# A two-block transformer kernel in fp32 on one core: a ninth weight slot, new buffers in the expert stage, and another order of ScalarE's work

## What is computed

```
def reference(...):
    x = first_block(x, ...)      # 2 x: x + hybrid_layer(x): one wide projection (3488 columns), four mixers
                                 #      (latent attention, short convolution, spatial gate, block attention),
                                 #      each gated by silu, and a projection back
    return second_block(x, ...)

def second_block(x, c, ...):
    c_act = silu(c)
    for i in range(2):
        sh1, sc1, g1, sh2, sc2, g2 = split(c_act @ ada_w[i] + ada_b[i])        # ada_w: 1024 x 6144
        h = x * (1 + sc1) + sh1
        y = neighbourhood_mixer(h, ...) if i == 0 else gqa_mixer(h, ...)       # 16 heads of 64
        x = layer_norm(ALPHA * x + (1 + g1) * y, ln_g[i, 0], ln_b[i, 0])
        h = x * (1 + sc2) + sh2
        y = hierarchical_moe(h, ...)                                           # 32 experts, 2 per token
        x = layer_norm(ALPHA * x + (1 + g2) * y, ln_g[i, 1], ln_b[i, 1])
    return x
```

## Time and profile before

| | |
|---|---|
| median of 3 runs | 1589.41 us (1588.25 to 1590.89) |
| the profiled execution, its own time | 1588.65 us |
| its span, first to last instruction | 1586.9 us |
| PE, DVE, ACT, POOL busy | 88%, 36%, 14%, 6% of the span |
| moved by DMA | 533.32 MB, mean 336 GB/s |
| mean granted TensorE clock | 0.945 |

### The profile page before, as it was taken

One profiled execution on the slowest core, in us unless ns is written; L12 is line 12 of the kernel. 1 busy time (PEld: TensorE's weight loads), 2 busy tenths in 40 slices (PEclk: granted clock), 3 DMA queues, 4 the chain that ended last, 5 costly groups with the idle time before them and its releaser, 6 DMA issues.

```text
span 1586.9 us, 28389 instructions
## 1 busy us (share of the span) xinstructions
PE 1397.0 (88%) x12800; PEld 885.6 (56%) x12800; DVE 568.5 (36%) x1230; ACT 219.4 (14%) x578; POOL 87.9 (6%) x95
## 2 busy tenths in 40 slices
PE   7999999998998989789789788868998797897795
PEld 4885488577885555345445344447654554554442
DVE  3696569556835101101101115684211011111113
ACT  2230214011432000000000002332100000000000
POOL 3100111000003000000000001100200000000000
PEclk9999999999998999889989898989899998999999
DMA  9656846776856999999999998346799999999995
GB/s 346 235 196 237 299 163 209 249 287 226 301 223 259 427 426 426 427 427 426 427 428 424 425 372 295 105 160 267 295 425 427 427 425 427 425 428 425 426 419 199
DMA packets 96856, 533.32 MB, mean 336 GB/s; under 512 B 5184, under 2 KB 7424, under 8 KB 73168
## 3 DMA queue, kind: packets, MB, share of 16 engines
q1 hardware_dynamic: 92992, 519.40, 81.2%
q0 software_dynamic: 3728, 11.95, 2.2%
HBM read 530.28 MB, written 1.05 MB: 335 GB/s over the span
## 4 chain that ended last, share of the span: by engine, by line
PE 64%; DMA 25%; DVE 7%; ACT 2%; issue 1%; SPq 1%; DVEq 0%; ACTq 0%
PE bk L429 25%; DMA AR<-in_moe_w_down 24%; PE bk L892 18%; PE bk L926 8%; PE bk L610 3%; PE bk L936 3%; PE bk L425 3%; DVE AR L1011 2%; ACT AR L1817 1%; PE bk L654 1%; PE bk L639 1%; DVE mpart L1019 1%; SPq L2300 1%; DMA ring<-in_w_in 1%; DMA ring<-in_ada_w 1%
## 5 line engine op out<-in xcount | busy, mean ns | idle before, releaser
L892 PE MATMUL bk<-ring,AR 128*32 128x128 f32 x5120 | 307.8, 409 | 4.2 <-DVE AR L1016 4.2
L892 PEld LDWEIGHTS bk<-ring,AR 128*32 128x32 f32 x5120 | 192.4, 127 | 103.0 <-DVE AR L1016 5.3
L1011 DVE TENSOR_TENSOR AR<-bk,AR 128x128 f32<-128x128 f32 (+2 forms) x106 | 41.3, 389 | 539.2 <-ACT AR L1817 467.0
L429 PE MATMUL bk<-ring,AR 128*128 128x256 f32 (+2 forms) x736 | 211.7, 445 | 9.0 <-DVE lsum L1011 3.0
L1817 ACT ACTIVATE AR<-bk 128x512 f32<-128x512 f32 (+4 forms) x178 | 71.9, 422 | 1014.2 <-PE bk L892 789.8
L926 PE MATMUL bk<-ring,AR 128*32 128x512 f32 x656 | 163.6, 719 | 37.0 <-DMA ring<-in_moe_w_down 37.0
L926 PE MATMUL bk<-AR 128*32 128x512 f32 x368 | 148.9, 715 | 46.7 <-DMA AR<-in_moe_w_down 45.9
L892 PE MATMUL bk<-AR 128*32 128x128 f32 x3072 | 187.3, 410 | 0.0
L429 PEld LDWEIGHTS bk<-ring,AR 128*128 128x128 f32 x736 | 140.5, 193 | 75.0 <-issue 54.4
L429 PE MATMUL bk<-AR,ring 128*128 128x256 f32 (+1 forms) x832 | 172.9, 367 | 7.1 <-DVE diag L1011 5.4
L429 PEld LDWEIGHTS bk<-AR,ring 128*128 128x128 f32 x832 | 149.0, 192 | 28.0 <-DVE diag L1011 5.8
(11 more groups left out here) (152 smaller groups left out, 968.6 us busy)
## 6 DMA issues: line engine op xcount, KB each, us to landing
ring<-in_moe_w_gate SPq DMA_DIRECT2D x48, 2048.0 KB, 24.6
ring<-in_moe_w_down SPq DMA_DIRECT2D x36, 2048.0 KB, 28.6
ring<-in_moe_w_up SPq DMA_DIRECT2D x32, 2048.0 KB, 20.2
AR<-in_moe_w_up SPq DMA_DIRECT2D x32, 2048.0 KB, 29.2
ring<-in_ada_w SPq DMA_DIRECT2D x24, 2048.0 KB, 11.0
AR<-in_moe_w_down SPq DMA_DIRECT2D x20, 2048.0 KB, 29.1
AR<-in_moe_w_gate SPq DMA_DIRECT2D x16, 2048.0 KB, 15.8
ring<-in_w_in SPq DMA_DIRECT2D x12, 2048.0 KB, 13.0
```

Source lines behind the costliest of these rows:

```text
L429: ins = eng.matmul(o, l, r, start=i == 0, stop=i == len(pairs) - 1)
L892: ins = eng.matmul(o[32 * f:32 * f + 32, 128 * m:128 * m + 128], XG[u][:, c, 32 * j:32 * j + 32], w[:, c, f::4], start=c == 0, stop=c == N ...
L1011: return eng.tensor_tensor(o, a, b, op)
```

## The change

- **Slot 8.** `EXTRA` is 4. The new slot lies at columns 12288 to 16384 of the arena; it is free once the last output unit, `o13`, has been made. The planner's dates are new. By its rule, in both layers, the gate/up pieces of experts 0 to 3 go to eight slots that are free ahead of the experts, as before, and the down piece of expert 0, which took the slot of the first gate piece, now takes slot 7.
- **Buffers.** `XH` moves to where `SEL` was; `SEL` is now two small pairs, one for each parity of q, made by `select(i, q)` a quad at a time: quad 0 in `router`, quad q + 1 behind quad q's `GST` copy.
- **Norm rows.** `LNG` is gone. The norm ahead of the experts borrows `XG[1]` (shift, loaded when the attention's last output bank has been read and both deviations are made) and `YS` (scale, loaded only when the second half of the raw tokens is complete, `raw`). So `gather(1)` and the first down product wait for `fin`. `finish` waits for quad 0's selection and not for all. The rows of the norm behind the experts go into `XG`, and are loaded when the last gate/up bank of quad 6 and of quad 7 is made.
- **ScalarE's order.** In `attend` a round's exponentials come ahead of the copies of the round before; `settle` runs behind them.
- **Side work.** In na two "+" move from round 2 to round 6. In gqa sum 20 is made ahead of the attention and extracted in round 0, and three banks instead of one serve the side work one round earlier. In the mixers one silu ("Sa") moves a round earlier.

```
-EXTRA = 3
+EXTRA = 4
...
-FILL = ... ("a0",), ("a1", "Sc"), ("b1", "tot", "Sa"), ...
+FILL = ... ("a0",), ("a1", "Sc", "Sa"), ("b1", "tot"), ...
...
-NA_SIDE = ((), ("x13", "+", "+"), ("x14", "+", "+", "+", "+"), ("x15", "+", "+"), ("x16", "+", "+"), ("x17", "+", "+"),
-           ("m",), ("l", "o00"), ("o01",), ("o02", "o03", "s"))
+NA_SIDE = ((), ("x13", "+", "+"), ("x14", "+", "+"), ("x15", "+", "+"), ("x16", "+", "+"), ("x17", "+", "+"),
+           ("m", "+", "+"), ("l", "o00"), ("o01",), ("o02", "o03", "s"))
...
-GQA_ROUNDS = (("q01",), ("r10",), ("q11",), ("r01", "t20"), ("t21",), ("r11",),
+GQA_ROUNDS = (("q01",), ("r10",), ("q11",), ("r01",), ("t21",), ("r11",),
...
-GQA_SIDE = (("v10",), ("w10",), ("v01", "+", "w01"), ("+",), ("v11", "+", "w11"), ("x20", "+"), ...
+GQA_SIDE = (("x20", "v10"), ("w10",), ("v01", "+", "w01"), ("+",), ("v11", "+", "w11"), ("+",), ...
...
-            for k, when in enumerate((519, 521, 541)):
+            for k, when in enumerate((486, 487, 510, 505)):
...
-                    for k, when in enumerate((100, 104, 128)):
+                    for k, when in enumerate((95, 96, 128, 122)):
...
                 for f in ("k0", "k1", "q00", "K0", "K1", "q10", "r00"):
                     unit(f)
+                    if f == "q00":
+                        total(20, next_bank())
...
-                    if len(todo) == 2:
+                    if len(todo) == 3:
                         fill_bank[0] = [7, 0, 1]
...
-        XH = view(A_SS, NT, D)
-        SEL = [view(A_EE + 1024 * t, NE, CAP) for t in range(NT)]
+        XH = view(A_EE, NT, D)
+        SEL = [[view(A_ROWS + 1024 + 256 * u + 128 * t, 4, CAP) for t in range(NT)] for u in range(2)]
...
+        LN_IN = YS, view(A_ET + 1024, D)
+        LN_OUT = view(A_ET, D), view(A_ET + 1024, D)
...
+            def select(i, q):
+                for t in range(NT):
+                    ins = tt(SEL[q % 2][t], bcast(cst[:, K_IOTA:K_IOTA + CAP], 1, 4),
+                             bcast(R_PM[:, t, 4 * q:4 * q + 4], 2, CAP), ALU.is_equal)
+                    if t:
+                        v.tell(ins, sem("sel"), 8 * i + q + 1)
+                    else:
+                        v.step(ins)
...
-                for e0, ne in ((0, 4), (4, NE - 4)):
-                    for t in range(NT):
...
+                select(i, 0)
...
                         free(eng.tensor_copy(GST[u], bank("gsT", i, q)[:, 0:256]), "gsT", i, q)
+                        if q + 1 < NQ:
+                            select(i, q + 1)
...
                 def gather(q):
                     v.wait_ge(*filled("xg", i, q, 1))
+                    if q == 1:
+                        v.wait_ge(sem("fin"), i + 1)
...
+                        if not q:
+                            v.wait_ge(sem("fin"), i + 1)
...
+                    if i:
+                        settle()
                     if i >= 3 and tag in TAG:
                         outputs(tag, i - 3)
...
-                    settle()
+                settle()
...
+            def norm_before(i):
+                g.wait_ge(*drained("o", TAG[i], 7))
+                norm_row(2 * i, 1, LN_IN[1])
+                g.wait_ge(sem("raw"), 2 * i + 2)
+                norm_row(2 * i, 0, LN_IN[0])
+
+            def norm_after(i):
+                for n in range(2):
+                    g.wait_ge(*filled("gu", i, NQ - 2 + n, 3))
+                    norm_row(2 * i + 1, n, LN_OUT[n])
...
-                g.wait_ge(sem("sel"), 2 * i + 2)
+                g.wait_ge(sem("sel"), 8 * i + 1)
...
             deviation(0)
-            g.wait_ge(*drained("o", "na", 7))
-            norm_rows(0)
             deviation(1)
+            norm_before(0)
             finish(0)
-            g.chain()
-            norm_rows(1)
+            norm_after(0)
...
+                DONE["arena", 3] = filled(TAG[i], "o13")
```

More of the change, by code:

```diff
@@ L46 @@
 PLAIN = (("v", 0), ("s", 0))
-FILL = tuple((("qk0",), ("qk1",) + one, ("v0",), ("v1", "tot"), ("s0",), ("s1", "Sd"), ("a0",), ("a1", "Sc"),
-              ("b1", "tot", "Sa"), ("b0",), ("g1", "tot"), ("g0",), ("spat", "tot", "Sb")) for one in ((), ("tot",)))
+FILL = tuple((("qk0",), ("qk1",) + one, ("v0",), ("v1", "tot"), ("s0",), ("s1", "Sd"), ("a0",), ("a1", "Sc", "Sa"),
+              ("b1", "tot"), ("b0",), ("g1", "tot"), ("g0",), ("spat", "tot", "Sb")) for one in ((), ("tot",)))
 MIX_SIDE = tuple(((), one, (), ("ext", "v1"), (), (), ("s1", "svar", "ada", "bd"), ("a0", "svn", "ada"),
@@ L870, in gather @@
                                           [(XH[:, t, 128 * (4 * b + cc):128 * (4 * b + cc) + 128],
-                                            SEL[t][:, 4 * q:4 * q + 4, :].rearrange("p e s -> p (e s)")) for t in range(NT)])
+                                            SEL[q % 2][t].rearrange("p e s -> p (e s)")) for t in range(NT)])
                         end(ins, "xg", i, q, b)
@@ L1627, in router @@
                 v.chain()
-                for e0, ne in ((0, 4), (4, NE - 4)):
-                    for t in range(NT):
-                        ins = tt(SEL[t][:, e0:e0 + ne, :], bcast(cst[:, K_IOTA:K_IOTA + CAP], 1, ne),
-                                 bcast(pm[:, t, e0:e0 + ne], 2, CAP), ALU.is_equal)
-                        if t:
-                            v.tell(ins, sem("sel"), 2 * i + 1 + (e0 > 0))
-                        else:
-                            v.step(ins)
+                select(i, 0)
                 for t in range(NT):
@@ L2107, in gather @@
                     s.wait_ge(*filled("xg", i, q, 0))
+                    if q == 1:
+                        s.wait_ge(sem("fin"), i + 1)
                     if q > 1:
@@ L2184, in layer_loads, with norm_row @@
                 small(sgw, A["sg_w"][l], f"lay{l}")
-            def norm_rows(k):
-                small(LNG[:, 0, :], A["ln_g"][k // 2, k % 2:k % 2 + 1, :].to_broadcast([P, D]), f"row{k}")
-                small(LNG[:, 1, :], A["ln_b"][k // 2, k % 2:k % 2 + 1, :].to_broadcast([P, D]), f"row{k}")
+            def norm_row(k, n, dst):
+                small(dst, A[("ln_g", "ln_b")[n]][k // 2, k % 2:k % 2 + 1, :].to_broadcast([P, D]), f"row{k}")
+            def norm_before(i):
[7 more added lines that the diff above has]
+                    norm_row(2 * i + 1, n, LN_OUT[n])
             n_var = [0]
@@ L2205, in finish @@
                     g.step(tt(x[t], XH[:, t, :].rearrange("p (c k) -> p k c", c=NC),
-                              LNG[:, 0, :].rearrange("p (k c) -> p k c", c=NC), ALU.mult))
+                              LN_IN[0].rearrange("p (k c) -> p k c", c=NC), ALU.mult))
                 g.chain()
-                g.step(tt(X[:, 0, :], X[:, 0, :], LNG[:, 1, :], ALU.add))
-                g.tell(tt(X[:, 1, :], X[:, 1, :], LNG[:, 1, :], ALU.add), sem("fin"), i + 1)
+                g.step(tt(X[:, 0, :], X[:, 0, :], LN_IN[1], ALU.add))
+                g.tell(tt(X[:, 1, :], X[:, 1, :], LN_IN[1], ALU.add), sem("fin"), i + 1)
             def first_layer(l):
@@ L2280, in _ @@
             deviation(0)
-            g.wait_ge(*drained("o", "gqa", 7))
-            norm_rows(2)
             deviation(1)
+            norm_before(1)
             finish(1)
-            g.chain()
-            norm_rows(3)
+            norm_after(1)
             for t in range(NT):
```

42 lines of the change are left out of this document (21 added, 21 removed).

## The result

The changed kernel takes **1563.94 us**, median of four runs (1561.59 to 1565.4), beside 1589.29 for the kernel before on the same chip (1588.25 to 1590.89): ratio 0.9838, 95% interval 0.9821 to 0.9855, so 25.4 us faster. The forecast was 1560.5, in a range from 1552 to 1571. The profiled execution took 1563.89, its span is 1562.2.

A forecast was written before the change was run, and what follows sets the result against it. Expert stages were taken as bound by the DMA stream, everything ahead of them by computing. 9.8 + 3.9 + 7.8 + 11.1 - 4.0 = 28.6 off 1588.65 gives 1560.05, on the median 1560.8; forecast 1560.5, range 1552 to 1571.

The forecast's parts named there:

- Ninth slot: Start of each expert stage: one more 2 MB load runs in the stream's hole, 4.9 us per layer, 9.8 in all.
- The rows of the last norm: Expert stages: these rows travel later but inside the saturated stream, ahead of its last bytes, at no cost.
- Router, 3.9: Layer 0's router: some 2 for the two comparisons and 2.6 of 2.82 leave the chain, 3.9 us; layer 1 nothing.
- First attention, 7.8: VectorE's late modulation piece and TensorE's gap of 5.39 go; 64 matmuls take 10.64, not 13.01: 7.8 us.
- Second attention, 11.1: Shorter waits for numerators, sum 20 moved, an output bank of its own: 5.1 + 1.2 + 1.1 + 1.8 - 1.1 + 3.0.
- Mixers, 0: Mixers: ScalarE switches tables twice less per layer, but nobody waits for it there, so nothing is gained.
- GpSimd's norm, minus 2 per layer: Start of expert stages: the norm now lies over the first gate products; bounds 0 and 4 per layer, middle taken.
- rival of the full stop: Both products wait for the end of a GpSimd operation, up to 4.5 together, in both layers: 4 more, 1564; 10%.
- copies that hold TensorE: Attentions: copies behind the exponentials make TensorE wait for banks; slower, 1624, or 1600 if half the rounds do; 3%.
- the prefetch alone: Both attentions keep their length and only the prefetch counts: 9.8 + 3.9 - 4 = 10, so 1579; 9%.
- half of the second attention's gain: Second attention: rotation and scores waiting for a transposed query eat the first round's gain, about 6 less, 1566; 22%.
- the norm's overlap costs nothing: Expert starts: rows land sooner or products fall between GpSimd's operations, and the mixers give a microsecond: 1555; 18%.

The follow-up runs named there:

- third profile with both: Changed kernel with GpSimd's norm later and quad 0's down products first, plus ScalarE's old order in the first attention: 1558.66 us.
- second execution: The changed kernel measured and profiled again without any edit: 1566.0 us, ratio 0.9844 to the kernel before.

## Why the prediction was right

**Ninth slot, 4.9 per layer: right in kind, a fifth too high.** Between two kernels that differ in the slot and in when GpSimd's norm starts, and in whose expert stages nothing is held, it gives 3.7 and 4.0.

**The rows of the last norm, nothing: wrong.** They were to travel later at no cost. With three slots and the rest of the change the expert stages are 1.2 and 0.9 longer than before, and their stream dips at the end of quad 0. TensorE finishes quad 0's gate and up products at 522.8 and makes no down product that frees a slot until 534.8; between them lie 3.7 of gathering for quad 1 that could wait. The wait was as long in the kernel before, but there the queue had 1 MB more to move. With the down products first the dip is gone, and the stages are 2.1 and 0.9 shorter than with GpSimd's norm later alone (1.7 and nothing in the third profile with both). The forecast took every hole but the one at the start for covered.

**Router, 3.9: right in size, wrong in its cause.** It was split into 2 for the comparisons and 2.6 for `over`. The comparisons cost nothing that shows; GpSimd held `mod` too, which stood in the trace with 1.15 instead of 0.17 and wasn't read.

**First attention, 7.8: right.** 7.2 and 5.6 in the whole change, 7.9 alone.

**Second attention, 11.1: right as a sum of two terms that were off in opposite directions.** The order was put at 7.4 (5.1, 1.2 and 1.1) and gave 4.7 alone. The sum and the bank were put at 3.7 and gave 7.1. In the whole change the stage was 11.0 and 14.8 shorter, and what sets it between 130.1 and 134.0 stays open. A wait of TensorE was priced at its length and not with the low clock of the matmuls behind it, though for the gap in the first attention that very step was made.

**Mixers, 0: right for the change, though not for the one execution that was read.** The profiled execution of before was quick there where twelve of fourteen aren't. Between profiled executions these 3.3 are nearly all that is missing. Whether they also explain why the median is 1563.94 and not 1560.5 isn't shown: the forecast was held against the median of before too, which is no single execution, and stage lengths are known for profiled ones only. The later medians of before, 1590.2 to 1590.7, are about 1 above the one that the forecast used.

**GpSimd's norm, minus 2 per layer: right in mechanism, but there is no value around 2.** Four profiled kernels have the collision, so eight stages. In six the products begin ahead of GpSimd's second pair and take 0.7 to 1.4, the comparisons behind them are held for up to 3.9, and the stage is within 1 us of those in which nothing is held. In two (layer 1 of the second execution, layer 0 of the kernel with the down products first) the products begin just behind that pair, are held for over 4, the stream pauses, and the stage is 4.3 and 3.2 longer. So the cost is nearly nothing or about 4. The forecast's 4 for the sum was too much for the first execution, where by luck it made up for the slot and the rows, and right for the second. The held operations ended within 0.2 of an end of GpSimd's (504.18 and 504.04 in the rows above, 1109.33 and 1109.17 in the second execution). "SBUF — State Buffer" of the Trainium skill, section "SBUF: two separate sides", says that a VectorE operation with two SBUF inputs and a GpSimd operation that reads SBUF exclude each other for a whole instruction, and these ends agree with it. The rival of the full stop, 1564, gives the measured time, but not by its mechanism: it has the gate products stopped in both layers, and no execution shows that in more than one.

The rivals of copies that hold TensorE, of the prefetch alone and of half of the second attention's gain fall by the stage table. The rival that the norm's overlap costs nothing holds for six stages of eight, though its 1555 didn't come. That a slot is worth nothing falls by the run with three.

**Still open.** What ScalarE's order is worth inside the changed kernel: its stage says 4 to 8, the median of the run without it 1.5 or nothing. Whether the norm's rows, put back, would fill the dip at the end of quad 0. Not tried: a layout in which the first slot returns before 493, which is what is left of the hole.

## What to carry to other kernels

When a transfer is moved out of a busy stream, look for the next place where the consumer frees no slot for longer than the loads in hand last: the transfer may have been what kept the queue busy there. Putting the consumer's slot-freeing work first cleared such a place here. Background work on GpSimd should be put over VectorE operations that read matmul banks, and moved by an explicit wait rather than by when its rows happen to land: here one index in a wait kept every product at 0.48, in a kernel that otherwise lost nearly nothing in some stages and about 4 us in others. Take the base of a sum from several executions, since one part of a kernel can differ by 3 to 5 us between them; look at the same stages before a difference of medians is put down to an edit. And price a wait of TensorE with the matmuls behind it.

## What the runs showed of the hardware

The granted clock could fall in two stretches of the mixers with the same instructions: from 165 to 175 us it was 0.83 or 0.84 in twelve of fourteen executions and 1.00 in two, from 10 to 20 it was 0.83 in six and 1.00 in eight. In four of those eight the first 48 matmuls still took 21.1 to 21.3, against 18.3 in the others and 20.0 at 0.83. The same pair of products took 0.66 where it began 0.39 ahead of GpSimd's second pair (layer 0 of the second execution), and 4.51 where it began 0.33 behind it. And a small operation is held as long as a large one: 128x8 took 1.15, and 2.46 in the kernel with three slots, instead of 0.17.
